# Hybrid decoder step on one core: the third qkv chunk computed in three groups of token tiles, with the first two attention items inside it

## The reference

```python
proj = h @ w_qkv                       # 1024 -> 1024 queries, 256 keys, 256 values
q = rope_partial(rmsnorm(q, q_norm), pos)
k = rope_partial(rmsnorm(k, k_norm), pos)
# prompt: blocks of 128 queries look at their own and the previous 128 keys
# samples: 8 queries look at 128 cached keys and the 8 new ones
s = einsum('...qkgd,...skd->...kgqs', qg, k) * 64 ** -0.5
s = where(mask, s, -inf)
m = maximum(s.max(-1), sink)
p = exp(s - m)
denom = p.sum(-1) + exp(sink - m)
o = einsum('...kgqs,...skd->...qkgd', p / denom, v)
y = o @ w_out
```

## Time and profile before

| | us |
|---|---|
| median of 3 runs (lowest, highest) | 1193.08 (1192.41, 1193.56) |
| the profiled execution's own time | 1195.07 |
| its span | 1193.2 |
| PE busy in the span | 1176.5 (99%) |
| DVE busy | 887.4 (74%) |
| ACT busy | 631.7 (53%) |

### The profile page before, as it was taken

One profiled execution on the slowest core, in us unless ns is written; L12 is line 12 of the kernel. 1 busy time (PEld: TensorE's weight loads), 2 busy tenths in 40 slices (PEclk: granted clock), 3 DMA queues, 4 the chain that ended last, 5 costly groups with the idle time before them and its releaser, 6 DMA issues.

```text
span 1193.2 us, 24075 instructions
## 1 busy us (share of the span) xinstructions
PE 1176.5 (99%) x9572; PEld 892.4 (75%) x9572; DVE 887.4 (74%) x1327; ACT 631.7 (53%) x1051; POOL 172.7 (14%) x289
## 2 busy tenths in 40 slices
PE   8999999999999999999999999999999999999998
PEld 6865777877777777777774456777777777787886
DVE  5887677586888878777774479757788878787655
ACT  6446455366555555454445469846555555544432
POOL 2000010002223222000003300000222222210001
PEclk9999999999999999999999999999999999999999
DMA  9605453235555455445646310023656456345663
GB/s 283 181 2 159 119 154 95 76 104 153 151 132 144 113 131 149 122 122 146 155 111 228 102 53 2 3 71 108 167 126 162 110 126 155 88 127 140 158 174 78
DMA packets 197626, 148.60 MB, mean 125 GB/s; under 512 B 5905, under 2 KB 178763, under 8 KB 197474
## 3 DMA queue, kind: packets, MB, share of 16 engines
q1 hardware_dynamic: 181392, 101.72, 29.5%
q0 software_dynamic: 16064, 45.68, 16.6%
q10 hardware_dynamic: 90, 0.09, 0.0%
HBM read 109.15 MB, written 9.86 MB: 100 GB/s over the span
## 4 chain that ended last, share of the span: by engine, by line
PE 83%; DVE 7%; DMA 3%; ACT 3%; issue 2%; SPq 1%; DVEq 0%; ACTq 0%; POOLq 0%
PE PS L653 33%; PE PS L875 17%; PE PS L809 15%; PE PS L669 6%; PE PS L1603 3%; DMA stage<-in_w_ffn_up 1%; DMA stage<-stage 1%; DVE wL L363 1%; DVE P L2904 1%; SPq L2954 1%; DVE xT L701 1%; DVE st L2885 1%; DMA rowsF<-in_ffn_conv_b 1%; PE PS L1775 1%; ACT ntmp L709 1%
## 5 line engine op out<-in xcount | busy, mean ns | idle before, releaser
L875 PE MATMUL PS<-hidH,blk 128*128 128x288 f16 x1232 | 227.9, 286 | 0.4 <-ACT val L598 0.4
L363 DVE SCALAR_TENSOR_TENSOR wL<-stage,wH 128x1024 f16<-128x1024 f32 x136 | 165.1, 1219 | 51.6 <-ACT wH L357 51.1
L357 ACT ACTIVATE wH<-stage 128x1024 f16<-128x1024 f32 x136 | 142.0, 1048 | 91.1 <-PE PS L653 50.4
L875 PE MATMUL PS<-hidL,blk 128*128 128x288 f16 x616 | 176.2, 286 | 0.0
L653 PE MATMUL PS<-zH,wH 128*128 128x288 f16 x832 | 169.9, 286 | 0.7 <-DVE zL L714 0.7
L653 PE MATMUL PS<-zL,wH 128*128 128x288 f16 x832 | 169.8, 286 | 0.0
L653 PE MATMUL PS<-zH,wL 128*128 128x288 f16 x832 | 169.8, 286 | 0.0
L875 PEld LDWEIGHTS PS<-hidH,blk 128*128 128x128 f16 x1232 | 120.5, 98 | 30.9 <-ACT val L598 0.7
L653 PEld LDWEIGHTS PS<-zH,wH 128*128 128x128 f16 x832 | 81.2, 98 | 22.0 <-DVE zL L714 1.3
L653 PEld LDWEIGHTS PS<-zH,wL 128*128 128x128 f16 x832 | 81.4, 98 | 20.5
L653 PEld LDWEIGHTS PS<-zL,wH 128*128 128x128 f16 x832 | 81.4, 98 | 20.5
(11 more groups left out here) (487 smaller groups left out, 2550.1 us busy)
## 6 DMA issues: line engine op xcount, KB each, us to landing
stage<-in_w_ffn_up SPq DMA_DIRECT2D x88, 512.0 KB, 4.3
quart<-in_w_ffn_down SPq DMA_DIRECT2D x32, 704.0 KB, 5.4
stage<-stage POOLq DMA_DIRECT2D x54, 256.0 KB, 4.9
stage<-in_w_mlstm_in SPq DMA_DIRECT2D x20, 512.0 KB, 6.4
stage<-in_w_swa_qkv SPq DMA_DIRECT2D x12, 512.0 KB, 4.7
quart<-quart POOLq DMA_DIRECT2D x8, 704.0 KB, 5.3
quart<-mixed POOLq DMA_DIRECT2D x8, 704.0 KB, 5.6
C<-in_state_mlstm_C POOLq DMA_DIRECT2D x4, 1024.0 KB, 6.7
```

Source lines behind the costliest of these rows:

```text
L357: nc.scalar.activation(wH[:, slot, :], stage[:, slot, :], ACT.Copy, scale=WSCALE).then_inc(hi_ready, inc)
L363: nc.vector.scalar_tensor_tensor(out=wL[:, slot, :], in0=stage[:, slot, :], scalar=WSCALE, in1=wH[:, slot, :], op0=ALU.mult, op1=ALU.subtr ...
L875: m = nc.tensor.matmul(down_bank(g), blk[:, g % RING, a, 128 * k:128 * (k + 1)], (hidH, hidL)[b][:, k, HIDDEN[j], :], start=(k == 0 and (a ...
```

## The change

Four edits.

1. **Chunk 2 in three groups of tiles.** PE runs the four units for tiles 0, 1 and 2 (`EARLY_TILES`), then the four for tile 3, then the four for tile 4. `unit_used` is still told behind tile 4. The groups that stood ahead of units 0, 1 and 2 still stand ahead of them, those that stood ahead of unit 3 (7, 8, 9) now stand behind the early tiles.
2. **Items 0 and 1 inside.** `scores(0)` stands behind the first unit of tile 3, `scores(1)` behind the second unit of tile 4. ACT and DVE have the exponentials, maxima and divisions of these items between the tiles' copies. Group 12 is the last of `BEFORE_UNIT`; group 13 stands behind `turn(0)`.
3. **The sout splits later.** Units 0 and 1 are split between tile 3 and tile 4, unit 2 at item 16 and unit 3 at item 17 (`LATE_SPLITS`).
4. **Copies of cached keys sooner on ACT.** Groups 0 and 1 are copied ahead of the split of chunk 2's unit 3, not behind it. `rms(2)` moves from the start of attention to item 1.

```diff
-        BEFORE_UNIT = ((0, 1), (2, 3), (4, 5, 6), (7, 8, 9), (10, 11, 12, 13))
+        BEFORE_UNIT = ((0, 1), (2, 3), (4, 5, 6), (7, 8, 9), (10, 11, 12))
+        EARLY_TILES = (0, 1, 2)
...
-        LATE_SPLIT = NI - 1
+        LATE_SPLITS = {NI - 2: 2, NI - 1: 3}
...
+            for c in range(2):
+                for u in range(4):
+                    qkv_unit(c, u, range(TT))
+            for u in range(4):
+                for g in BEFORE_UNIT[u] if u < 3 else ():
+                    group(g)
+                qkv_unit(2, u, EARLY_TILES)
+            for g in BEFORE_UNIT[3]:
+                group(g)
+            pe.wait_ge(masks_in, 1)
+            for u in range(4):
+                qkv_unit(2, u, (3,))
+                if u == 0:
+                    scores(0)
+            for u in range(4):
+                qkv_unit(2, u, (4,))
+                if u == 1:
+                    scores(1)
...
             groups_turned = []
-            scores(0)
-            scores(1)
...
                 turn(x)
+                if x == 0:
+                    group(13)
...
+                for tt in range(TT):
+                    qkv_tile(c, tt)
+                for g in BEFORE_UNIT[0] if c else ():
+                    group_evac(act, g)
+                split_act(act, ahead(unit("qkv", c, 3)))
+
+            rms(1)
+            for u in range(1, 3):
+                for g in BEFORE_UNIT[u]:
+                    group_evac(act, g)
+            act.wait_ge(asem["rope"], 2)
+            for tt in EARLY_TILES:
+                qkv_tile(2, tt)
+            for g in BEFORE_UNIT[3]:
+                group_evac(act, g)
+            exps(0)
+            qkv_tile(2, 3)
+            split_act(act, ahead(unit("qkv", 2, 0)))
+            split_act(act, ahead(unit("qkv", 2, 1)))
+            exps(1)
+            qkv_tile(2, 4)
...
+            for tt in EARLY_TILES:
+                qkv_tile(tt)
+                squares_summed(tt)
+            maxima(0)
+            normalise(0)
+            qkv_tile(3)
+            squares_summed(3)
+            split_dve(dve, ahead(unit("qkv", 2, 0)))
+            maxima(1)
+            split_dve(dve, ahead(unit("qkv", 2, 1)))
+            normalise(1)
+            qkv_tile(4)
```

More of the change, by code:

```diff
@@ L1893, in group @@
                 m.then_inc(asem["tr"], 1)
[L1895 to L1922, removed]
             def scores(x):
@@ L2297, in rms @@
                 m.then_inc(asem["rs"], 1)
[L2299 to L2329, removed]
             def exps(x):
@@ L2348, in exps, with qkv_tile @@
                 nc.scalar.activation(s[:, 5, :], s[:, 3, :], ACT.Exp).then_inc(asem["e"], 1)
+            def qkv_tile(c, tt):
+                normed_cols = 256 if c == 0 else 512
+                tm_done(act, "qkv", c, tt)
+                r = ROWS[tt]
+                for part in range(len(tm_parts(tt))):
+                    src, dst, cols = qkv_part(c, tt, part)
+                    wide = min(normed_cols, cols.stop) - cols.start
+                    if wide > 0:
+                        m = nc.scalar.activation(sqx(tt)[0:r, cols.start:cols.start + wide], tm_parts(tt)[part][0][:, 0:wide],
+                                                 ACT.Square, scale=rcol[0:r, tt:tt + 1])
+                    if c < 2:
+                        m = nc.scalar.activation(dst, src, ACT.Copy, scale=rcol[0:r, tt:tt + 1])
+                m.then_inc(asem["sq"] if c == 2 else free["qkv"], 1)
+            act.wait_ge(asem["cz"], 2)
+            for c in range(2):
+                for u in range(3):
+                    if c and u == 0:
+                        rms(c - 1)
+                    split_act(act, ahead(unit("qkv", c, u)))
+                    if c == 0 and u == 0:
+                        column_rstd()
+                if c:
+                    act.wait_ge(asem["rope"], c)
+                for tt in range(TT):
[18 more added lines that the diff above has]
+            qkv_tile(2, 4)
             def out_high(x):
@@ L2366, in _ @@
                     group_evac(act, 13)
+                    rms(2)
                 if x in BESIDE_ITEM:
                     group_evac(act, BESIDE_ITEM[x])
-                if x == LATE_SPLIT:
-                    split_act(act, ahead(unit("qkv", 2, 3)))
+                if x in LATE_SPLITS:
+                    split_act(act, ahead(unit("qkv", 2, LATE_SPLITS[x])))
                 if x >= 2 and late(x - 2):
@@ L2844, in _ @@
             link("V", dve, m)
[L2845 to L2867, removed]
             def maxima(x):
@@ L2905, in normalise, with qkv_tile @@
                                             ALU.mult).then_inc(asem["p"], 1)
+            def qkv_tile(tt):
+                dve.wait_ge(asem["sq"], tt + 1)
+                for part in range(len(tm_parts(tt))):
+                    src, dst, _ = qkv_part(2, tt, part)
+                    m = nc.vector.tensor_scalar(dst, src, rcol[0:ROWS[tt], tt:tt + 1], None, ALU.mult)
+                m.then_inc(free["qkv"], 1)
+            steps = iter(())
+            for c in range(2):
+                next(steps, None)
+                for u in range(4):
+                    split_dve(dve, ahead(unit("qkv", c, u)))
+                    next(steps, None)
+                steps = norm_rope(c)
+                if c == 0:
+                    dve.wait_ge(dMask, 16)
+                    nc.vector.tensor_copy(mask16[:, :], masks).then_inc(masks_in, 1)
+            for _ in steps:
+                pass
+            for tt in EARLY_TILES:
[10 more added lines that the diff above has]
+            qkv_tile(4)
             def scaled(x):
@@ L2919, in out_low @@
                 nc.vector.tensor_tensor(cols(hnL), src, cols(hnH), ALU.subtract).then_inc(asem["ol"], 1)
-            maxima(0)
-            maxima(1)
-            squares_summed(3)
             squares_summed(4).then_inc(asem["rss"], 1)
-            normalise(0)
             for x in range(NI):
-                if x == LATE_SPLIT:
-                    split_dve(dve, ahead(unit("qkv", 2, 3)))
+                if x in LATE_SPLITS:
+                    split_dve(dve, ahead(unit("qkv", 2, LATE_SPLITS[x])))
                 if x + 2 < NI:
                     maxima(x + 2)
-                if x + 1 < NI:
+                if 0 < x < NI - 1:
                     normalise(x + 1)
```

26 lines of the change are left out of this document (23 added, 3 removed).

## The result

The changed kernel takes **1195.09 us** (median of 20 runs, 1193.13 to 1197.51), the kernel before 1193.0 us in 20 runs on the same chip (1190.81 to 1194.3). Their ratio is 1.0018, 95% interval 1.0012 to 1.0024: 2.1 us slower, which lies within the 0.2% that the prediction called no change. The forecast was 1194.6 us, 1.5 us above before, with a range of 1192.4 to 1196.5. The time, the bound and the three waits that were named came out as forecast. What the sum set at nothing, a fall of the clock behind the new wait, was there too in the profiled execution.

A forecast was written before the change was run, and what follows sets the result against it. PE was taken as the bound: 2.0 us new idle less 1.1 gained left it 0.9 us late at item 4, 1.6 at item 5. Carrying +1.5 through attention gave 1193.08 + 1.5 = 1194.6 us, range 1192.4 to 1196.5.

The forecast's parts named there:

- the three waits that were named: PE waits: 2.0 us at group 5, 0.9 us ahead of item 4's scores, and lateness at item 5's scores (719.6).
- the sum: Total over the kernel: +1.5 us on the median 1193.08, giving 1194.6 us; no clock loss included.
- Part 1: Third chunk, group 5's transposes: PE waits for ACT's copy of group 2, queued behind `rms(1)`; 2.0 us new idle.
- The rival of the clock: Units 2 and 3 behind group 5's wait: idle lowers PE's clock, 1.5 us more (up to 1.75), 1196.1; chance 0.16.
- a clock below 1.00 behind the wait: Sign that the forecast is wrong: PE's granted clock falls behind group 5's wait; 1.00 was expected from 685 to 695.
- Part 2: To item 4's scores: at 715.6 against 714.71, PE 0.9 us late; DVE's two sout splits keep the gain small.
- The first wait of the earlier trace: PE's 0.88 us idle ahead of item 2's scores, waiting for ACT's exponentials; claimed hidden by the change.
- Part 3: Item 5's scores: `rms(2)` ahead of item 3's exponentials makes PE 1.6 us late at 719.6; +1.5 us carried through attention.
- Growing lateness: Rival, later attention items: DVE and ACT lack room to return to step, another 1 us, 1195.6; chance 0.10.
- Part 4: Later splits of sout units 2 and 3: hidden with 0.75 us to spare, set at nothing; at worst 0.3 us.
- No wait at group 5: Rival, third chunk: ACT copies group 2 by 685.4, all later steps 2.0 us earlier, 1192.6; chance 0.10.
- the free start: Rival, start of attention: no group 5 wait, splits hidden; PE gains 1.95 us and 0.4 us, 1190.7; chance 0.04.

The follow-up runs named there:

- e1: The changed kernel with ACT's copies of groups 2 and 3 ahead of `rms(1)`; 1192.25 us, ratio to the kernel before 0.9991.
- e2: The changed kernel with 16 useless transposes on PE ahead of group 5, filling the wait; 1195.47 us, ratio to the kernel before 1.0015.
- e4: `e1` with the splits of sout units 0 and 1 moved to items 12 and 14; 1195.43 us, ratio to the kernel before 1.0018.
- e8: `e1` with `rms(2)` behind item 3's exponentials and item 2's maxima ahead of tile 4's square sums on DVE; 1192.60 us, ratio to before 0.9989.
- e7: The changed kernel with 8 useless transposes on PE ahead of group 5, half as many as `e2`; 1195.15 us, one run.
- e6_all: `e1` with sout splits 0 and 1 at items 12 and 14 and `rms(2)` behind item 3's exponentials; 1195.12 us, ratio to before 1.0016.
- e0: The changed kernel once more, unchanged, as yardstick for the follow-up runs; 1196.15 us, ratio to the kernel before 1.0023.

## Why the prediction was right, point by point

- **The number.** 1195.09 against 1194.6 us. The waits in it were priced well. That the clock's fall, left out of the sum, did not carry the median further is luck: at least 9 of 27 executions did not have it, and an execution with all of it costs 1.7 us more.
- **Part 1, the wait at group 5.** Forecast 2.0 us at 685.4, which is 682.65 in this execution's time (2.75 us earlier). Measured: 2.01 us from 682.69. The cause, copies queued behind `rms(1)`, is shown by `e1`.
- **The rival of the clock.** Chance 0.16, price 1.5 us on top, 1.75 at most. Its mechanism was there in both profiles, at 1.7 us, and "a clock below 1.00 behind the wait" was one of the prediction's own signs of being wrong. So the step that failed is the sum's silence on it: I gave weight to the fact that the start's idle came early and this one amid gapless work. The Trainium skill ("TensorE: Matmul & The Clock Gate", "Why this matters for your kernels") advises against longer gaps between bursts than the one here; a reader would take 2.01 us as safe, and by the granted clock of 0.92 in 682 to 704 it was not. Had the forecast carried it in full it would have been 1196.3, above the median: 2.1 us measured lies between 1.5 and 3.2. How often the clock falls stays open, but for the 9 of 27 executions that can't have had the whole of it.
- **Part 2, item 4.** Forecast 0.9 us late, wait at 715.6, or 712.85 in this execution's time; it came at 714.67, 1.8 us later: the clock's 1.7. Without the clock (`e2`) it takes 39.85 us from the opening to item 4 against 38.81 before, 1.04 late. The first wait of the earlier trace rows, 0.88 us, is gone as predicted: no row of PE has a wait ahead of item 2. But the reason given for the small gain was half right. The two splits cost 0.48 us, and not ahead of item 4 but ahead of the turn of item 0 (`e4`); tile 4's square sums ahead of item 2's maxima held 0.6 us of the wait ahead of item 4 (`e8`). Splits and sums were both in the working of the prediction ("copies and squares of tile 4 ... until 711.9"), and I named one of them alone.
- **Part 3, item 5.** Forecast 0.7 us more lateness at item 5 by `rms(2)` ahead of item 3's exponentials. Measured: 3.91 us from item 4 to item 5 instead of 3.28, 0.63 more, a wait of 0.50, and 0.5 us back when `rms(2)` moves. The time forecast, 719.6, is 716.85 in this execution; 718.58 is 1.7 us later, the clock's again. Carried through attention: S without the clock is +1.55 (`e2`, `e7`), against +1.5.
- **Growing lateness.** It did not grow. From the scores of item 6 to the last value products it takes 781.74 - 722.29 = 59.45 us, before 781.25 - 721.82 = 59.43. The scores of item 6, before and after:

```profile
721.82 0.61 PE L1935 MATMUL PS<-mask,ident 128*128 128x512 bf16 x2
```

```profile
722.29 0.60 PE L1907 MATMUL PS<-mask,ident 128*128 128x512 bf16 x2
```

- **Part 4.** The same 59.45 against 59.43 us contain the later splits of output units 2 and 3: nothing, as forecast.
- **No wait at group 5, and the free start.** Both need the order of `e1` and the runs built on it. With it the price named for the first, 0.5 us under before, is about right: S 0.73 us shorter. The free start's 2.4 us were not reached by any version; `e8` comes nearest, with S 1.55 us shorter.

These are the PE waits after, from the view of waits (engine, waited for, us in total, times, longest). The first was predicted whole, the third in both its parts:

```profile
PE PS L1891 <- ACT kTT L1415: 2.0, 1, 2.0
PE PS L1991 <- DVE P L2907: 1.5, 3, 0.8
PE PS L1907 <- ACT st L2331: 1.4, 2, 0.9
```

## What to carry to other kernels

When work on the bounding engine is cut into shorter pieces, look for the instruction in the other engines' queues that was just in time for the longer pieces: here a small activation that waits for another engine had some 2 us of room and stood ahead of the copies that free PE's bank. Put what frees a buffer ahead of what waits, and what the bounding engine needs next ahead of sums that are read later. And price a new idle of two microseconds on PE twice, once as a wait and once as a fall of the clock that may follow it.

## What the runs showed of the hardware

- An idle of 2.01 us in a stretch of products without a gap was followed by 3.4 us at 1.2 GHz in both profiles of the changed kernel (pitch 0.43 us for 0.22), 1.7 us lost on 2.0 us of idle. With the wait filled by useless transposes the clock stayed at 1.00, and so it did with 1.14 us of idle (one profile each).
- The length of the idle alone does not decide. At the kernel's start, 1.20 us in `e7` was followed by a fall (clock 0.73 in 5 to 10; eight transposes take 1.89 us), while 1.68 us in `e4` was not (clock 1.00 in 10 to 15; eight transposes take 1.09 us). The rows of `e7`, then that of `e4`, stand below. What else decides was not tested.

```profile
5.62 1.07 PE L1498 MATMUL PS<-C,xtok 128*128 128x128 f32 x8 [1.20 <-DMA xtok<-in_x_prompt]
...
7.21 1.89 PE L1498 MATMUL PS<-C,xtok 128*128 128x128 f32 x8
```

```profile
11.80 1.09 PE L1498 MATMUL PS<-C,xtok 128*128 128x128 f32 x8 [1.68 <-DMA xtok<-in_x_prompt]
```

- In `e6_all` the clock fell to 0.66 in 760 to 765 with no idle longer than 0.81 us within the 20 us around it. What PE did just before were small products (128*32 128x64, the row of 758.46). The kernel before has the same products from 758.88 and no fall there, so they do not do it by themselves; whether they weigh on the clock was not tested.
- The clock averaged over a whole execution can rule a fall out and not prove one: `e1` had its eleven runs between 0.996 and 1.000, and the one at 0.996 took 1192.25 us, its median. Nor does the average hold all: at the start of `e0` the view of busy time gives 1.00 for 5 to 10 us, while eight transposes that take 1.06 us in `e4` (at 5.16) take 1.94 us (at 7.22). S leaves the start out.
